# One 128-column projection for the forget gate, the rotary key and its swapped copy

## The chip, the cores and the metric

The kernel runs on one core of a Trainium2 chip. The metric is the device time of one execution in microseconds (us). Before the change three executions took 2214.09, 2215.44 and 2216.43 us; the median is 2215.44 us. The profiled execution took 2216.96 us.

## The reference, cut to what matters

Two networks run one after the other. The first has two layers (`DEPTH = 2`) over 256 tokens of width 1024. Each layer begins like this:

```python
u = rms_norm(x, g_mix[l]) * (1 + sc_a) + sh_a
proj = u @ w_in[l]
fox_qkv, fox_f, mla_ql, mla_kvl, mla_kr, sb_qkv, gate_logit = jnp.split(proj, SPLIT_POINTS, axis=-1)
log_f = jax.nn.log_sigmoid((fox_f + b_fox_f[l]).astype(jnp.float32)).transpose(0, 2, 1)   # 8 columns
y_fox = merge_heads(fox_attention(fq, fk, fv, log_f))      # uses cumsum(log_f) over the tokens
...
k_rope = apply_rope(mla_kr, cos, sin)                      # 32 columns, shared by all 8 heads
y_mla = merge_heads(mla_attention(q_nope, q_rope, k_nope, k_rope, mla_v))
```

`fox_f` has 8 columns and `mla_kr` 32. The rotation is x1*cos - x2*sin next to x1*sin + x2*cos, so the kernel needs `mla_kr` once as it is and once with its two halves swapped. The cumulative sum of `log_f` is first needed by the scores of the first attention; the rotated key is needed by the second attention, later still. The second network (a neighbourhood attention with a gated branch, then a retention layer, each with a feed-forward part) is not touched.

## The kernel before, in words

All weights of both networks lie in HBM as one tape of 518 panels. A panel is 8 tiles of 128x128 float32 (512 KB), in the order in which TensorE uses them. The panels go through a ring of 7 slots (`RING`). For each panel SP issues the DMA once TensorE has released the slot (L912, counter `panel_used`); ScalarE (ACT) copies it to its rounded part `ring_r` (L1468, float32r); VectorE (DVE) computes the rest `ring_l = ring - ring_r` (L2041); then TensorE may use it. The first three panels are rounded and parted by GpSimd (POOL, L927 and L929). One weight tile costs three matmuls of 256 columns: rest times rounded activation, rounded times rounded, rounded times rest of the activation (L969, L972, L973 in `linear`, L1008, L1011, L1012 in `linear_abreast`, L988, L991, L992 with 512 columns in `stream`, which computes the value matrices).

Each engine runs its own instruction list in a fixed order written out by hand. TensorE's groups of one layer are named by `order_block1`; group g writes PSUM bank g mod 8, and waits until the group eight places earlier is freed (`FREED`). A group such as `fox_qk3` is one output tile of 128 features by 256 tokens: 8 weight tiles, so one panel and 24 matmuls.

A layer of the first network starts in this order on TensorE: `fox_f` (8 real columns of its 128, written twice, at partitions 0 and 64), `fox_qk0` and `fox_qk1` abreast, which means that their tiles alternate while the normalised input arrives part by part; `fox_qk2` to `fox_qk7`; `fox_v` (4 panels); `lat0` to `lat4`; `k_rope` (the 32 key columns, four copies side by side); `k_swap` (the same with halves swapped); two short statistics (L1079); `sb_qk0` to `sb_qk7`; `sb_v`; further projections of the latents; then the first scores.

DVE parts the panels in this order of its own: `ahead(name)` parts all panels up to six (`AHEAD`) past the one at which the named group starts. Between them DVE does the adaptive modulation of the next half: `ada` multiplies a 512 KB tile loaded by POOL (L938, two slots) with a vector and sums (L2066). Five of these stand before `fox_v`, four in the `lat` groups, five in the `sb_qk` groups.

For the forget gate ACT takes Abs, Exp and Ln of the bank (L1536, L1539, L1541) at the start of the layer, and DVE adds the bias and clips (L2215) and scans along the tokens (L2219). Both wait for `fox_f` at that place of their lists. In the first layer DVE then computes the rotary angles (L2079 to L2092) and the product of the condition (L2094), which needs ACT's sigmoid of 128x2048 elements (L1472, L1474, L1476); after it ACT loads another table for two sines and loads the first one back. The key is rotated by two products of bank and table (L2200) and one sum (L2203), each on 128 partitions.

ACT copies each finished group out of PSUM (L1514 for the queries and keys, L1554 and L1555 for the latents) and rounds the panels behind it: `finished(name)` waits for a group and rounds the panels that replace what the group before it had read.

Of the kernel before, what the change touches and what calls it, by code (L numbers as in the profile page):

```python
# [32 lines left out]
ACT = mybir.ActivationFunctionType  # L33
ALU = mybir.AluOpType
AX = mybir.AxisListType

P = 128
# [35 lines left out]
FOX_ROWS = 64 + H  # L73
# [4 lines left out]
TILES_1 = (KD + 3 * 4 * KD + KQ * KD + KKV * KD + 2 * KD + 3 * 4 * KD + (4 + 2 + 2) * KQ + 8 * KKV  # L78
           + 3 * KD * KD + 3 * KD * WT + KD * KD + 2 * FT * KD + KD * FT)
PANELS_1 = -(-TILES_1 // TILES_PER_PANEL)  # L80
assert PANELS_1 % RING == 0
# [116 lines left out]
def tape_block1(i, l):  # L198
# [6 lines left out]
    f_pad = np.zeros((D, P), np.float32)  # L205
    f_pad[:, :H] = f_pad[:, 64:FOX_ROWS] = sec[1]
    qk = stationary(sec[0][:, :2 * W])
    out += [abreast(stationary(f_pad), qk[:KD], qk[KD:2 * KD]), qk[2 * KD:], streaming(sec[0][:, 2 * W:])]
# [3 lines left out]
    out += [stationary(np.tile(kr, (1, 4))), stationary(np.tile(kr[:, swap], (1, 4)))]  # L212
# [98 lines left out]
def order_block1():  # L311

    o = ["stat_mix", "fox_f"] + [f"fox_qk{f}" for f in range(2 * WT)] + ["fox_v0", "fox_v1"]
    o += [f"lat{f}" for f in range(KQ + KKV)] + ["k_rope", "k_swap", "stat_q", "stat_kv"]
    o += [f"sb_qk{f}" for f in range(2 * WT)] + ["sb_v0", "sb_v1"]
    o += [f"mla_q{f}" for f in range(WT)] + [f"q_{n}{f}" for n in ("rope", "swap") for f in range(2)]
    o += [f"score{n}" for n in heads(0)]
    o += [f"mla_k{f}" for f in range(WT)] + ["mla_v0", "mla_v1"]
    o += [f"score{n}" for n in heads(1)]
    for p in range(1, PAIRS + 2):  # L320
        if p <= PAIRS:
            o.append(f"gate{2 * p - 2}")
        if p - 1 > STICKS:
            o.append(f"pv{p - 2}")
        if branch_at(p) is not None:
            o += [f"branch{branch_at(p)}_{f}" for f in range(KD)]
        if p <= PAIRS:
            o += [f"keys{n}" for n in heads(p - 1)] + [f"gate{2 * p - 1}"]
        if p + 1 < PAIRS:
            o += [f"score{n}" for n in heads(p + 1)]  # L330
        if p <= STICKS:
            o.append(f"pv{p - 1}")
    o += [f"w_out{f}" for f in range(KD)] + ["stat_ffn"]
    for f in range(FT):
        o += [f"ffn_gate{f}", f"ffn_up{f}"]
    return o + [f"down{f}" for f in range(KD)]
# [41 lines left out]
def two_blocks(nc, tape, ada_first_in, adas, consts, par1, cond_in, pos_in, x_in, par2_in, misc_in, ctx_in, bias_in,  # L378
               sgu_w_in, sgu_b_in, axial, dist_in, mask_in, out):
    n_panels = tape.shape[0]  # L380
    assert n_panels % RING == 0
# [6 lines left out]
    with ExitStack() as ctx:  # L388
# [109 lines left out]
        FOX = place(2 * WT, T)  # L498
        fox_qk, fox_v = at(FOX, 2 * WT, T), carve(2, W)
# [6 lines left out]
        log_keep, log_beta = at(FOX, 4, 3 * P), at(FOX + 12 * P, 4, 3 * P)  # L506
# [110 lines left out]
        cum_made = signal("cum_made", 1)  # L617
# [39 lines left out]
        FREED = {"stat_mix": (log_mean, 0), "fox_f": (fox_low, 0), "k_rope": (rope_mul, 0), "k_swap": (rope_mul, 1),  # L657
# [231 lines left out]
        def _(sp):  # L889
# [18 lines left out]
            with sp.Fori(1, n_panels // RING) as turn:  # L908
                for s in range(RING):
# [3 lines left out]
                        .then_inc(landed[s], 16)  # L913
            quarter = KD // 4
# [8 lines left out]
        def _(pool):  # L923
# [7 lines left out]
            pool.wait_ge(*done("fox_f", 0))  # L931
# [16 lines left out]
        def _(pe):  # L948
# [76 lines left out]
            for l in range(DEPTH):  # L1025
# [89 lines left out]
                project("k_rope", uk)  # L1115
                project("k_swap", uk)
# [13 lines left out]
                def scores(p):  # L1130
# [320 lines left out]
        def _(act):  # L1451
# [9 lines left out]
            def round_panels(n):  # L1461


                while made[0] < n:
                    q = made[0]
                    made[0] += 1
                    act.wait_ge(landed[q % RING], base[0] // RING * 16 + 16 * (q // RING + 1))
# [21 lines left out]
            for l in range(DEPTH):  # L1489
# [35 lines left out]
                if l == 0:  # L1525
# [9 lines left out]
                act.wait_ge(*done("fox_f", l))  # L1535
                act.activation(fox_l[0:FOX_ROWS, :], bank("fox_f")[0:FOX_ROWS, 0:T], ACT.Abs, bias=par_of("b_fox")[0:FOX_ROWS, :])\  # L1536
                    .then_inc(fox_soft.sem, 1)
                act.wait_ge(*fox_soft(0, l))
                act.activation(fox_l[0:FOX_ROWS, :], fox_l[0:FOX_ROWS, :], ACT.Exp, scale=-1.0).then_inc(fox_soft.sem, 1)  # L1539
                act.wait_ge(*fox_soft(1, l))  # L1540
                act.activation(fox_l[0:FOX_ROWS, :], fox_l[0:FOX_ROWS, :], ACT.Ln, bias=1.0).then_inc(fox_soft.sem, 1)  # L1541
                finished("fox_f")
# [14 lines left out]
                finished("k_rope")  # L1557
                finished("k_swap")
# [479 lines left out]
        def _(dve):  # L2038
# [97 lines left out]
            for l in range(DEPTH):  # L2136
# [69 lines left out]
                if l == 0:  # L2206
# [5 lines left out]
                ahead("fox_f", l)  # L2212
                dve.wait_ge(*done("fox_f", l))
                dve.wait_ge(*fox_soft(0, l))
                dve.tensor_scalar(fox_t[0:FOX_ROWS, :], bank("fox_f")[0:FOX_ROWS, 0:T], par_of("b_fox")[0:FOX_ROWS, :], 0.0, ALU.add, ALU.min)\  # L2215
                    .then_inc(fox_low.sem, 1)
                dve.wait_ge(*fox_low(0, l))
                dve.wait_ge(*fox_soft(2, l))
                dve.tensor_tensor_scan(neg_cum[0:FOX_ROWS, :], fox_l[0:FOX_ROWS, :], fox_t[0:FOX_ROWS, :], 0.0, ALU.add, ALU.subtract)\  # L2219
                    .then_inc(cum_made.sem, 1)  # L2220
# [8 lines left out]
                if l == 0:  # L2229
                    rope_angles()  # L2230
# [7 lines left out]
                rotate(0, "k_rope", "k_swap", k_rope)  # L2238
# [612 lines left out]
```

## Time and profile before

| | |
|---|---|
| median of three executions | 2215.44 us |
| profiled execution | 2216.96 us |
| its span, first to last instruction | 2214.9 us |
| outside the span | 2.1 us |
| PE / PEld / DVE / ACT / POOL busy | 2086.2 / 1861.9 / 1601.8 / 1160.1 / 106.8 us |
| instructions PE / DVE / ACT | 13692 / 2625 / 2049 |
| mean granted TensorE clock | 0.979 |
| DMA, tape panels | 518 of 512 KB, median 3.3 us from issue to landing |
| DMA, modulation tiles | 176 of 512 KB, median 4.6 us |

PE is TensorE's matmuls, PEld its weight loads, DVE VectorE, ACT ScalarE, POOL GpSimd, SP SyncE. Matmuls overlap one another, so the duration of one is not its price; the price is the distance between the starts of two. A wait "A <- B" means that A's engine was idle before A and that B ended this. The first layer's projections start at about 40 us and the second's at about 535 us; the first network ends at about 1036 us.

### The profile page before, as it was taken

Reading aid. Unit: us, or ns where it says so; the run is one execution under the profiler, and the core shown is the slowest. Engines: PE = TensorE matmul, PEld = TensorE weight load, DVE = VectorE, ACT = ScalarE, POOL = GpSimd, SP = SyncE. Lnnn points to the kernel's source line nnn. Section 1 sums busy time; section 2 is a strip of 40 time slices with the busy share of each in tenths; the row PEclk is TensorE's granted clock in tenths of the full one; section 3 lists DMA queues with packets and bytes.
Section 4 is the critical chain, followed back from the end, with each engine's and each line's share of the span. In section 5 each row is a group of like instructions: output and inputs, shape, how many; then the busy total and the mean of one; then the engine's idle time right before and its main releaser. Section 6 shows DMA issues by size and latency. Waiting matters only on the chain.

```text
span 2214.9 us, 36264 instructions
## 1 busy us (share of the span) xinstructions
PE 2086.2 (94%) x13692; PEld 1861.9 (84%) x13692; DVE 1601.8 (72%) x2625; ACT 1160.1 (52%) x2049; POOL 106.8 (5%) x186
## 2 busy tenths in 40 slices
PE   3999999999999989998997999999998999998998
PEld 3989999999988989997874668787876888998998
DVE  7778868955778868945876778677877526657983
ACT  3657746645457746645636355353434225656762
POOL 2000000000000000000000100001100000000000
PEclk9999999999999999999998999999999999999999
DMA  8766546854766546855440524546553322243553
GB/s 333 264 232 206 179 159 218 270 189 153 265 225 213 172 162 226 289 170 179 135 162 1 190 86 144 179 133 198 192 190 105 104 95 96 95 144 124 187 185 105
DMA packets 107469, 385.08 MB, mean 174 GB/s; under 512 B 11696, under 2 KB 16432, under 8 KB 106032
## 3 DMA queue, kind: packets, MB, share of 16 engines
q1 hardware_dynamic: 78880, 284.32, 37.9%
q0 software_dynamic: 25344, 92.29, 12.2%
q10 hardware_dynamic: 3088, 6.29, 0.8%
q8 instruction: 109, 1.79, 0.3%
q14 instruction: 48, 0.39, 0.1%
HBM read 381.81 MB, written 1.05 MB: 173 GB/s over the span
## 4 chain that ended last, share of the span: by engine, by line
PE 87%; DVE 7%; ACT 3%; issue 1%; DMA 1%; DVEq 0%; SPq 0%; ACTq 0%
PE ps L969 22%; PE ps L973 22%; PE ps L972 22%; PE ps L988 3%; PE ps L991 3%; PE ps L992 3%; PE ps L1008 2%; PE ps L1011 2%; PE ps L1012 2%; DVE ada_junk L2066 2%; PE ps L1275 1%; PE ps L1418 1%; DVE ring_l L2041 1%; PE ps L1202 1%; DVE work L2467 1%
## 5 line engine op out<-in xcount | busy, mean ns | idle before, releaser
L969 PE MATMUL ps<-part,ring_l 128*128 128x256 f32 (+1 forms) x3568 | 1098.1, 308 | 19.7 <-DVE part L2041 15.4
L973 PE MATMUL ps<-part,ring_r 128*128 128x256 f32 (+1 forms) x3568 | 1084.6, 304 | 0.0
L972 PE MATMUL ps<-part,ring_r 128*128 128x256 f32 (+1 forms) x3568 | 1082.9, 304 | 0.0
L1468 ACT ACTIVATE ring_r<-ring 128x1024 fp32r<-128x1024 f32 x515 | 535.4, 1057 | 450.1 <-DMA ring<-tape_in 332.1
L2041 DVE TENSOR_TENSOR ring_l<-ring,ring_r 128x1024 fp32r<-128x1024 f32 x515 | 622.2, 1220 | 195.8 <-ACT ring_r L1468 193.1
L969 PEld LDWEIGHTS ps<-part,ring_l 128*128 128x128 f32 x3568 | 672.8, 189 | 62.3 <-DVE part L2041 20.2
L972 PEld LDWEIGHTS ps<-part,ring_r 128*128 128x128 f32 x3568 | 675.6, 189 | 30.4 <-issue 1.2
L973 PEld LDWEIGHTS ps<-part,ring_r 128*128 128x128 f32 x3568 | 671.8, 188 | 28.8
L2066 DVE SCALAR_TENSOR_TENSOR ada_junk<-work 128x1024 bf16<-128x1024 f32 x272 | 337.7, 1242 | 49.2 <-DMA work<-adas_in 36.8
L1008 PE MATMUL ps<-part,ring_l 128*128 128x256 f32 (+1 forms) x240 | 79.6, 332 | 35.4 <-DVE part L2185 20.9
L988 PE MATMUL ps<-ring_l,part 128*128 128x512 f32 x264 | 105.3, 399 | 6.0 <-DVE part L2456 6.0
L991 PE MATMUL ps<-ring_r,part 128*128 128x512 f32 x264 | 104.8, 397 | 0.0
L992 PE MATMUL ps<-ring_r,part 128*128 128x512 f32 x264 | 104.7, 397 | 0.0
L2491 DVE SCALAR_TENSOR_TENSOR work<-ps,par,work 128x510 f32<-128x510 f32 (+1 forms) x88 | 53.9, 612 | 55.7 <-ACT work L1789 55.4
L938 POOL DMA_DIRECT2D work<-adas_in x96 | 50.9, 530 | 853.2 <-DVE ada_junk L2066 823.6
L1008 PEld LDWEIGHTS ps<-part,ring_l 128*128 128x128 f32 x240 | 51.2, 213 | 41.9 <-issue 39.6
L1789 ACT ACTIVATE work<-ps,par 128x512 f32<-128x512 f32 (+1 forms) x88 | 58.0, 660 | 42.7 <-PE ps L973 29.6
L1011 PE MATMUL ps<-part,ring_r 128*128 128x256 f32 (+1 forms) x240 | 78.0, 325 | 0.0
L1012 PE MATMUL ps<-part,ring_r 128*128 128x256 f32 (+1 forms) x240 | 78.0, 325 | 0.0
L944 POOL DMA_DIRECT2D work<-adas_in x80 | 42.3, 529 | 689.0 <-DVE ada_junk L2066 689.0
L2041 DVE TENSOR_TENSOR part<-work,part 128x256 fp32r<-128x256 f32 (+1 forms) x134 | 61.4, 470 | 10.1 <-ACT part L1926 3.9
L1476 ACT ACTIVATE work<-work 128x256 f32<-128x256 f32 (+2 forms) x138 | 64.6, 468 | 4.4
(226 smaller groups left out, 1947.7 us busy)
## 6 DMA issues: line engine op xcount, KB each, us to landing
ring<-tape_in SPq DMA_DIRECT2D x518, 512.0 KB, 3.3
work<-adas_in POOLq DMA_DIRECT2D x176, 512.0 KB, 4.6
work<-ada_first_in SPq DMA_DIRECT2D x8, 1024.0 KB, 13.2
work<-bias_in ACTq DMA_DIRECT2D x1, 2048.0 KB, 7.9
x<-x_t_in SPq DMA_DIRECT2D x1, 1024.0 KB, 15.6
work<-cond_in SPq DMA_DIRECT2D x1, 1024.0 KB, 18.2
x<-ctx_in ACTq DMA_DIRECT2D x1, 1024.0 KB, 7.6
x<-dist_in ACTq DMA_DIRECT2D x1, 1024.0 KB, 9.7
```

The source lines that it names most:

```text
L969: mm = pe.matmul(dst, lhsT=wl, rhs=mr, start=(k == 0), stop=False)
L972: pe.matmul(dst, lhsT=wr, rhs=mr, start=False, stop=False)
L973: mm = pe.matmul(dst, lhsT=wr, rhs=ml, start=False, stop=(k == len(moving) - 1))
L988: mm = pe.matmul(dst, lhsT=xr, rhs=wl, start=(k == 0), stop=False)
L991: pe.matmul(dst, lhsT=xr, rhs=wr, start=False, stop=False)
L992: mm = pe.matmul(dst, lhsT=xl, rhs=wr, start=False, stop=(k == n - 1))
L1008: mm = pe.matmul(dst, lhsT=wl, rhs=mr, start=(k == 0), stop=False)
L1011: pe.matmul(dst, lhsT=wr, rhs=mr, start=False, stop=False)
L1012: mm = pe.matmul(dst, lhsT=wr, rhs=ml, start=False, stop=(k == len(moving) - 1))
L1468: act.activation(ring_r[:, q % RING, :], ring[:, q % RING, :], ACT.Copy).then_inc(rounded, 1)
L2041: return dve.tensor_tensor(dst, whole, rounded_part.bitcast(F32), ALU.subtract)
L2066: dve.scalar_tensor_tensor(ada_junk[:, :], t, 1.0, vector, ALU.mult, ALU.mult, accum_out=sums).then_inc(sig.sem, 1)
```

## The change

`fox_f`, `k_rope` and `k_swap` become one group, `fox_rope`, that stands where `k_rope` stood. Its 128 columns are the key (0 to 31), the swapped key (32 to 63) and the forget gate (64 to 71); the rest is zero. `fox_qk0`, `fox_qk1` and `fox_qk2` now run abreast. The work of ACT and DVE on the forget gate moves behind the `lat` groups, and DVE rotates 32 partitions instead of 128 and adds four times, once for each copy of the result. The scanned row block of partitions 64 to 71 is copied to partitions 0 to 7. A layer has 145 panels in place of 147, so the tape has 514, no multiple of 7; the last three are issued behind SP's loop, and a slot's number follows from the whole tape and not from the layer.

```diff
-    out += [abreast(stationary(f_pad), qk[:KD], qk[KD:2 * KD]), qk[2 * KD:], streaming(sec[0][:, 2 * W:])]
+    out += [abreast(*(qk[f * KD:(f + 1) * KD] for f in range(ABREAST))), qk[ABREAST * KD:], streaming(sec[0][:, 2 * W:])]
-    out += [stationary(np.tile(kr, (1, 4))), stationary(np.tile(kr[:, swap], (1, 4)))]
+    fox_rope = np.zeros((D, P), np.float32)
+    fox_rope[:, 0:ROPE], fox_rope[:, ROPE:2 * ROPE], fox_rope[:, FOX] = kr, kr[:, swap], sec[1]
+    out += [stationary(fox_rope)]
...
-    o = ["stat_mix", "fox_f"] + [f"fox_qk{f}" for f in range(2 * WT)] + ["fox_v0", "fox_v1"]
-    o += [f"lat{f}" for f in range(KQ + KKV)] + ["k_rope", "k_swap", "stat_q", "stat_kv"]
+    o = ["stat_mix"] + [f"fox_qk{f}" for f in range(2 * WT)] + ["fox_v0", "fox_v1"]
+    o += [f"lat{f}" for f in range(KQ + KKV)] + ["fox_rope", "stat_q", "stat_kv"]
...
-        FREED = {"stat_mix": (log_mean, 0), "fox_f": (fox_low, 0), "k_rope": (rope_mul, 0), "k_swap": (rope_mul, 1),
+        FREED = {"stat_mix": (log_mean, 0), "fox_rope": (rope_mul, 1),
...
+            for n in range(n_panels // RING * RING, n_panels):                       # SP
+                sp.wait_ge(panel_used, n - RING + 1)
+                sp.dma_start(ring[:, n % RING, :], tape[n]).then_inc(landed[n % RING], 16)
...
-            pool.wait_ge(*done("fox_f", 0))
+            pool.wait_ge(*done("fox_qk0", 0))
...
-                slot = panel % RING                                                  # PE
+                slot = (base[0] + panel) % RING
...
-                project_abreast(["fox_f", "fox_qk0", "fox_qk1"], uk, lambda k: u_made(k, l))
-                for f in range(2, 2 * WT):
+                project_abreast([f"fox_qk{f}" for f in range(ABREAST)], uk, lambda k: u_made(k, l))
+                for f in range(ABREAST, 2 * WT):
                     project(f"fox_qk{f}", uk)
...
-                project("k_rope", uk)
-                project("k_swap", uk)
+                project("fox_rope", uk)
...
-                        pe.wait_ge(*cum_made(0, l))
+                        pe.wait_ge(*cum_made(1, l))
...
+                act.wait_ge(*done("fox_rope", l))          # ACT, behind lat4; Abs, Exp, Ln moved here
+                act.activation(fox_l[FOX, :], bank("fox_rope")[FOX, 0:T], ACT.Abs, bias=par_of("b_fox")[FOX, :])\
...
-                ahead("fox_f", l)                          # DVE, start of the layer; clip and scan moved
-                dve.wait_ge(*done("fox_f", l))
+                ahead("fox_qk0", l)
+                if l == 0:
+                    rope_angles()
...
-                rotate(0, "k_rope", "k_swap", k_rope)
+                ahead("fox_rope", l)
+                dve.wait_ge(*done("fox_rope", l))
+                dve.wait_ge(*fox_soft(0, l))
+                dve.tensor_scalar(fox_t[FOX, :], bank("fox_rope")[FOX, 0:T], par_of("b_fox")[FOX, :], 0.0, ALU.add, ALU.min)\
...
+                dve.tensor_tensor_scan(neg_cum[FOX, :], fox_l[FOX, :], fox_t[FOX, :], 0.0, ALU.add, ALU.subtract)\
...
+                dve.tensor_copy(neg_cum[0:H, :], neg_cum[FOX, :]).then_inc(cum_made.sem, 1)
+                straight, swapped, first = slice(0, ROPE), slice(ROPE, 2 * ROPE), bank("fox_rope")
+                dve.tensor_tensor(rope_t[straight, 0, :], first[straight, 0:T], rope_c[straight, :], ALU.mult).then_inc(rope_mul.sem, 1)
+                dve.tensor_tensor(rope_t[straight, 1, :], first[swapped, 0:T], rope_s[swapped, :], ALU.mult).then_inc(rope_mul.sem, 1)
+                dve.wait_ge(*rope_mul(1, l))
+                for n in range(4):
+                    add = dve.tensor_tensor(k_rope[n * ROPE:(n + 1) * ROPE, :], rope_t[straight, 0, :], rope_t[straight, 1, :], ALU.add)
+                add.then_inc(rope_made.sem, 1)
```

## Rows read from the trace of the kernel before

**Rows 1.** The page: busy time, and the engines of the chain that ended last.
```profile
PE 2086.2 (94%) x13692; PEld 1861.9 (84%) x13692; DVE 1601.8 (72%) x2625; ACT 1160.1 (52%) x2049; POOL 106.8 (5%) x186
...
PE 87%; DVE 7%; ACT 3%; issue 1%; DMA 1%; DVEq 0%; SPq 0%; ACTq 0%
```

**Rows 2.** Stretches: length; busy and instructions by engine; granted clock, DMA share, GB/s.
```profile
core 0: us, PE busy (x) PEld busy (x) DVE busy (x) ACT busy (x) POOL busy (x), PEclk, DMA share, GB/s
50.18:69.21 19.03, 17.67 (x146) 17.39 (x145) 14.80 (x22) 18.41 (x23) 1.51 (x3) 1.00 0.61 224
80.44:100.59 20.15, 20.15 (x170) 20.15 (x168) 15.65 (x19) 12.65 (x20) 2.08 (x4) 1.00 0.84 287
...
546.74:564.02 17.28, 17.28 (x146) 17.28 (x145) 12.72 (x15) 9.03 (x16) 1.58 (x3) 1.00 0.71 242
575.26:595.41 20.15, 20.15 (x169) 20.15 (x168) 14.46 (x18) 12.43 (x20) 1.98 (x4) 1.00 0.75 258
160.00:200.00 40.00, 39.70 (x327) 34.30 (x326) 36.74 (x86) 32.74 (x88) 3.70 (x7) 1.00 0.63 205
```

**Rows 3.** TensorE's waits from 40 to 300 us: total, times, longest.
```profile
PE ps L1202 <- DVE work L2330: 1.4, 1, 1.4
PE ps L969 <- DVE ring_l L2041: 1.4, 1, 1.4
```

**Rows 4.** Waits of all engines, 40 to 205 us.
```profile
ACT ring_r L1468 <- DMA ring<-tape_in: 13.0, 10, 2.8
...
DVE ada_junk L2066 <- DMA work<-adas_in: 8.0, 8, 2.1
DVE work L2192 <- PE ps L992: 6.6, 1, 6.6
```

**Rows 5.** Timeline of PE, ACT and DVE, 43 to 62 us: start, us, instruction, [idle before].
```profile
60.34 0.36 PE L969 MATMUL ps<-part,ring_l 128*128 128x256 f32 x1 [1.36 <-DVE ring_l L2041]
...
43.98 3.89 ACT L1468 ACTIVATE ring_r<-ring 128x1024 fp32r<-128x1024 f32 x4
...
50.93 1.90 ACT L1472 ACTIVATE work<-work 128x2048 f32<-128x2048 f32 x1
...
56.75 1.28 ACT L1547 ACT_TABLE_LOAD   x1
...
60.09 0.94 ACT L1514 ACTIVATE work<-ps 128x256 f32<-128x256 f32 x3
...
50.23 0.48 DVE L2215 TENSOR_SCALAR work<-ps,par 72x256 f32<-72x256 f32 x1 [1.60 <-ACT work L1536]
51.13 0.69 DVE L2219 TENSOR_TENSOR_SCAN work<-work 72x256 f32<-72x256 f32 x1 [0.42 <-ACT work L1541]
...
56.77 2.29 DVE L2094 TENSOR_TENSOR work<-work 128x2048 f32<-128x2048 f32 x1 [1.68 <-ACT work L1476]
58.98 1.22 DVE L2041 TENSOR_TENSOR ring_l<-ring,ring_r 128x1024 fp32r<-128x1024 f32 x1
62.00 1.23 DVE L2041 TENSOR_TENSOR ring_l<-ring,ring_r 128x1024 fp32r<-128x1024 f32 x1 [1.81 <-ACT ring_r L1468]
```

**Rows 6.** Timeline of DVE around the end of the values, and at the next ones.
```profile
77.88 1.23 DVE L2066 SCALAR_TENSOR_TENSOR ada_junk<-work 128x1024 bf16<-128x1024 f32 x1 [0.68 <-DMA work<-adas_in]
...
80.08 1.23 DVE L2041 TENSOR_TENSOR ring_l<-ring,ring_r 128x1024 fp32r<-128x1024 f32 x1
...
98.56 1.22 DVE L2066 SCALAR_TENSOR_TENSOR ada_junk<-work 128x1024 bf16<-128x1024 f32 x1 [1.39 <-DMA work<-adas_in]
```

**Rows 7.** DVE by line and shape, 40 to 150 us: count, busy us, mean ns, idle before.
```profile
L2041 DVE TENSOR_TENSOR ring_l<-ring,ring_r 128x1024 fp32r<-128x1024 f32 x37 | 44.3, 1221 | 7.7 <-ACT ring_r L1468 7.5
...
L2203 DVE TENSOR_TENSOR work<-work 128x256 f32<-128x256 f32 x3 | 1.3, 426 | 0.1
...
L2200 DVE TENSOR_TENSOR work<-ps,rope_c 128x256 f32<-128x256 f32 x3 | 1.3, 419 | 0.1
```

**Rows 8.** The stretch that follows a wait of TensorE of 1.4 us.
```profile
290.00:300.00 10.00, 9.05 (x63) 8.74 (x64) 5.84 (x11) 3.06 (x5) 0.02 (x1) 0.83 0.43 151
```

More of the change, by code:

```diff
@@ L72 @@
 STICKS = 2 * PER_BRANCH
-FOX_ROWS = 64 + H
+FOX = slice(64, 64 + H)
 ADA_BEFORE = {"fox_qk": 5, "lat": 4, "sb_qk": 5, "q_rope": 2}
@@ L380, in two_blocks @@
     n_panels = tape.shape[0]
-    assert n_panels % RING == 0
     cat, n_const = columns(shape_constants())
@@ L497, in two_blocks @@
         HIDDEN = taken[0]
-        FOX = place(2 * WT, T)
-        fox_qk, fox_v = at(FOX, 2 * WT, T), carve(2, W)
+        FOX_QK = place(2 * WT, T)
+        fox_qk, fox_v = at(FOX_QK, 2 * WT, T), carve(2, W)
         sb_qk, sb_v = carve(2 * WT, T), carve(2, W)
@@ L505, in two_blocks @@
         soft = at(LAT, 4, 3 * P)
-        log_keep, log_beta = at(FOX, 4, 3 * P), at(FOX + 12 * P, 4, 3 * P)
+        log_keep, log_beta = at(FOX_QK, 4, 3 * P), at(FOX_QK + 12 * P, 4, 3 * P)
         sigma = carve(SIGMAS, T)
@@ L616, in two_blocks @@
         fox_low = signal("fox_low", 1)
-        cum_made = signal("cum_made", 1)
+        cum_made = signal("cum_made", 2)
         qk_made = signal("qk_made", 4 * WT)
@@ L1464, in round_panels @@
                 while made[0] < n:
-                    q = made[0]
+                    q = base[0] + made[0]
                     made[0] += 1
-                    act.wait_ge(landed[q % RING], base[0] // RING * 16 + 16 * (q // RING + 1))
+                    act.wait_ge(landed[q % RING], 16 * (q // RING + 1))
                     act.activation(ring_r[:, q % RING, :], ring[:, q % RING, :], ACT.Copy).then_inc(rounded, 1)
@@ L1532, in _ @@
                 round_panels(RING)
[L1535 to L1542, printed above, removed]
                 if l == 0:
@@ L1556, in _ @@
                     finished(f"lat{f}")
-                finished("k_rope")
-                finished("k_swap")
+                act.wait_ge(*done("fox_rope", l))
+                act.activation(fox_l[FOX, :], bank("fox_rope")[FOX, 0:T], ACT.Abs, bias=par_of("b_fox")[FOX, :])\
+                    .then_inc(fox_soft.sem, 1)
+                act.wait_ge(*fox_soft(0, l))
+                act.activation(fox_l[FOX, :], fox_l[FOX, :], ACT.Exp, scale=-1.0).then_inc(fox_soft.sem, 1)
+                act.wait_ge(*fox_soft(1, l))
+                act.activation(fox_l[FOX, :], fox_l[FOX, :], ACT.Ln, bias=1.0).then_inc(fox_soft.sem, 1)
+                finished("fox_rope")
                 inverse_rms(1, "stat_q", MLA_Q, l)
@@ L2209, in _ @@
                 normalised(0, gs_mix, 0)
-                ahead("fox_f", l)
-                dve.wait_ge(*done("fox_f", l))
[L2214 to L2220, printed above, removed]
+                ahead("fox_qk0", l)
+                if l == 0:
+                    rope_angles()
                 ada_next = itertools.count()
@@ L2811 @@
             par1[:, l, a:a + w] = feature_major(v[l])
-        par1[:H, l, PAR1["b_fox"][0]] = par1[64:FOX_ROWS, l, PAR1["b_fox"][0]] = i["b_fox_f"][l]
+        par1[FOX, l, PAR1["b_fox"][0]] = i["b_fox_f"][l]
     par2 = np.zeros((P, DEPTH, N_PAR2), np.float32)
```

12 lines of the change are left out of this document (6 added, 6 removed).

## The prediction

> **What bounds the kernel now.** I read the page first: TensorE has matmuls in flight for 94% of the span, and 87% of the chain that ended last is PE [rows 1]. A busy PE can still be a slow one, because matmuls overlap, so I looked next at the stretches in which the three groups lie. From 80.44 to 100.59 us TensorE runs `lat0` to `lat4`, `k_rope` and `k_swap`: 7 groups of 24 matmuls, 168 in all (the row counts two that reach in). PE and PEld are busy for the whole 20.15 us. The same seven groups of the second layer take 20.15 us again [rows 2]. That is 2.879 us a group, or 119.9 ns from one matmul to the next, with two quite different DVE and DMA shares beside it. So in this part time is the number of matmuls times 120 ns, and nothing else.
>
> The queries and keys behind the abreast part (`fox_qk2` to `fox_qk7`) are 144 matmuls. In the second layer they take 17.28 us, 2.880 us a group. In the first they take 19.03 us less a gap of 0.12 to the next line, so 1.6 us more, and PE is busy for 17.67 us only [rows 2]. The waits say why: one of 1.4 us at L969 for a `ring_l` of DVE; between 40 and 290 us there is no other wait above 1 us inside the projections [rows 3]. Everything else that DVE, ACT and the DMAs do there is behind TensorE. DVE even stands 6.6 us waiting for the `sb_v` matmuls [rows 4].
>
> **The matmuls that go.** Per layer 24 tiles (`fox_f`, `k_rope`, `k_swap`) become 8. That is 16 tiles, 48 matmuls, two panels; twice, 96 matmuls and four panels. One group leaves ahead of `fox_v`: the abreast part keeps three groups and its pace is that of the arriving input, so the group is missing in the 120 ns part behind it, which has five groups in place of six. The other leaves behind `lat4`. Saved: 4 groups x 2.879 us = 11.5 us [rows 2]. The Trainium skill (TensorE: Matmul & The Clock Gate, Back-to-back issue gap) gives 262 cycles of 2.4 GHz, 109 ns, for an isolated gap of 256 columns; by it the 96 matmuls would be worth 10.5 us. The trace has 119.9 ns at the full clock, and the measurement decides.
>
> **The wait at 60.34 us in the first layer.** Its history is in the timeline [rows 5]. DVE clips and scans the forget gate from 50.23 to 51.82 us after standing 1.60 us for ACT's Abs and 0.42 us for the Ln; it computes the angles until 55.09; it stands 1.68 us for the sigmoid of the condition, which ACT could start only at 50.93, behind Abs, Exp and Ln; the product takes 2.29 us; only then, at 58.98, is panel 6 parted, until 60.20. TensorE wanted it at 50.18 + 3 x 2.88 = 58.8 us and got it at 60.34. The lost time is 1.5 us.
> After the change ACT is done with its four panels at 43.98 + 3.89 = 47.9 us and goes straight to the sigmoid, which takes 56.75 - 50.93 = 5.8 us, so until 53.7. DVE has its angles by then (3.3 us from 48.6). Product until 56.0, panel 6 until 57.2: 1.6 us ahead of need. What is late next is panel 7, for whose rounding DVE stands 1.81 us now too. ACT must first change tables and do the sines (60.09 - 56.75 = 3.3 us, to 57.0), then copy four groups instead of three (0.31 each, to 58.3), round panel 7 (1.0) and DVE part it (1.2): about 60.5, wanted at 61.7. Margin 1.2 us. Behind it the five modulation tiles come. The first starts 3.6 us earlier than now and each later one hangs on the landing of a load that the one before it let POOL issue, so the last ends 3.6 us earlier, at 75.5 instead of 79.1 [rows 6], while TensorE is 1.5 + 2.9 = 4.4 us earlier. The parting now at 80.08 to 81.3 serves a panel wanted at 83.3, so 2.0 us of margin become about 1.2. I count the full 1.5 us as saved; from the other side it is 0, if one of the two margins of 1.2 us is gone.
>
> **The forget gate and the rotation, moved and reshaped.** On ACT the three operations cost what they cost before, and two roundings of 1.05 us go. On DVE, per layer: two partings of 1.22 go (2.44 us), and of the rotation nothing but the number of adds changes, from one to four, plus one copy. No row shows an operation on 32 or 8 partitions. The nearest are the add on 128 partitions (0.426 us) and the clip on 72 (0.480 us) [rows 5, 7]; from below it is nothing, from above 0.69 us, the scan's. I take 0.43, as partitions seem not to enter: the clip on 72 costs no less than the product on 128 (0.419). So four operations more make 1.7 us, against 2.4 saved: DVE has 0.7 us less to do per layer (bounds: 2.4 less to 0.4 more). None of it stands on the path.
> But the block is one piece now: clip 0.48, scan 0.69, copy 0.43, two products 0.84, four adds 1.70, in all 4.1 us, and a wait for TensorE and ACT in front. Behind it in DVE's list stand all later partings, the normalisation of the latents and the `sb_qk` modulation tiles. `ahead("fox_rope")` has parted up to five panels past the group before, 5 x 2.88 = 14.4 us of work for TensorE. And DVE comes late: its last modulation tile in the `lat` groups ends now at 99.8 us [rows 6], 2.1 us after `k_rope` (97.7); after the change it moves up by 4 to 5 us, with two partings behind it, so the block begins some 4 us after `fox_rope` is finished. ACT is through with Abs, Exp and Ln by then (1.4 us [rows 5], behind one rounding). I cost the wait at nothing and the block at nothing. The lag this adds to DVE, some 4 us, is worked off in the 6.6 us in which it now waits for `sb_v` [rows 4]. The cumulative sum is needed at the first score, over 40 us later; if this cover were gone the price would be the block's 4.1 us.
>
> **The rest.** POOL's first modulation load waits for `fox_qk0` instead of `fox_f`, both the first group of the abreast part: nothing. SP's three loose issues are behind the same counter as in the loop: nothing. The banks turn by two places, but the distance of eight groups to the one freed is kept everywhere, and near the merged group the freed ones are over four groups (11 us) old: nothing. 2 MB of 385 less to load: nothing, as no transfer is on the path here.
>
> **Sum.** 11.5 + 1.5 = 13.0 us. Everything after the first scores is tied to TensorE and moves up with it. Against the profiled 2216.96 us (span 2214.9 and 2.1 around it) this is 2204.0; that execution is 1.5 us above the median, and against the median of 2215.44 it is 2202.4. I forecast 2202.4 us.
>
> **The rivals.**
> *The wait only moves.* The first layer's 1.5 us come back at panel 7 or behind the values, because both margins are 1.2 us and rest on landings that now vary (waits of DVE for modulation tiles up to 2.1 us [rows 4]). For it: ACT is busy for 18.41 of 19.03 us in that stretch [rows 2]. Then only the matmuls count: 2215.4 - 11.5 = 2203.9; with a new stall of 2 us in each layer, 2208.
> *Another engine has become the bound further on.* Between 160 and 200 us DVE is busy for 36.74 of 40 us [rows 2]. If it set the pace there, TensorE's lead would be lost in a wait, and only DVE's own saving, 0.7 us a layer, and part of the 1.5 would stay: 2213 to 2214, no change. Against it: PE waits 0.3 us in those 40 (39.70 busy), and DVE catches up with TensorE at `sb_v`, before this part.
> *The clock.* After the wait of 1.4 us near 290 us the granted clock is 0.83 over ten microseconds [rows 8], that is 3.4 us at 1.2 GHz in place of 2.4, which costs 1.7 us. Such stretches begin and end a few microseconds apart from run to run; a wait that goes can save one, a new one can add one: 1.7 us either way. It widens the range.
> *Slower: the moved block starves TensorE.* ACT's list is in order: the Abs stands behind roundings that wait for landings (2.8 us the longest here [rows 4]), DVE's block behind the Abs, the partings behind the block. It decides once DVE stands longer than the 14.4 us of parted panels. Every microsecond beyond that is lost in both layers; 6.5 us beyond cancel the gain, and at 25 us of standing, 10.6 lost per layer and a slow clock after each (1.7), the time is 2202.4 + 2 x 12.3 = 2227. Against it: the longest wait seen plus the whole block and ACT's three operations is 2.8 + 4.1 + 1.4 = 8.3 us.
> *The change doesn't do what it says.* If the compiled tape kept 518 panels, nothing would be saved; the trace would show 13692 matmuls again. I see no place where this could come from.
>
> **How the numbers follow.** Forecast, 2200.5 to 2204.5 by the spread of the three runs and the clock: 0.68. The wait moves, 2203.9 to 2208: 0.20. Absorbed further on or not made, 2211 to 2215: 0.05. More than forecast, to 2198, by slow-clock stretches that go: 0.05. Slower: 0.02. The range that holds 8 in 10 is 2199.5 to 2206.5; the bounds of DVE's small operations do not widen it, as they are covered. About 0.2%, 4.4 us, is what a measurement of this kernel tells from no change. Faster by more: 0.93; within: 0.05; slower: 0.02.
>
> **What would show it.** Matmuls 13596, panels 514. The run behind the abreast part is five groups long and takes 14.4 us in both layers, with no wait at L969; the run from `lat0` to the statistics takes 17.3 us. The first layer's `fox_v` starts 4.4 us earlier, the statistics 7.3 us earlier than at 100.59; the second layer's are 13 us earlier than at 595.4. DVE's block begins after `fox_rope` has ended and without idle time before the clip. The prediction is wrong if PE shows a wait above 1 us between 50 and 140 us, if the lead of 7 us at the statistics is smaller at the first `gate` groups, or if the groups cost other than 2.88 us.

## The result, and the profile after

The changed kernel took 2203.67 us (median of 6 executions) and the kernel before 2215.93 us (6) on the same chip. The ratio is 0.9933 with a 95% interval of 0.9913 to 0.9952: 14.8 us less, between 10.6 and 19.3. One disturbed execution of the changed kernel, far above the rest (2957.66 us), is left out of the ratio but stands among the 6; without it the median is 2202.98. The changed kernel was run twice more beside the experiments: 2202.08 us, ratio 0.9933 (0.9912 to 0.9955), and 2203.23 us, ratio 0.9946 (0.9927 to 0.9965). The forecast was 2202.4 us, 13.0 less than before. An interval of 10.6 to 19.3 us contains that, but it contains 11.5 as well; which terms are right has to come from the traces.

The changed kernel's page, the lines that answer to [rows 1], and its panels:

```profile
PE 2081.3 (94%) x13596; PEld 1856.5 (84%) x13596; DVE 1601.9 (72%) x2629; ACT 1156.6 (52%) x2045; POOL 107.0 (5%) x186
...
PE 86%; DVE 8%; ACT 3%; issue 1%; DMA 1%; DVEq 0%; SPq 0%; ACTq 0%
...
ring<-tape_in SPq DMA_DIRECT2D x514, 512.0 KB, 3.4
```

96 matmuls are gone, and PE is busy for only 4.9 us less than in [rows 1]. The clock of the two profiled executions hides the rest: the third profile of the changed kernel, which has a mean clock of 0.980, shows PE busy for 2072.8 us, 13.4 less than before. A mean granted clock of 0.979 over a span of 2214.9 us means 93 us at 1.2 GHz in place of 2.4. If the work of these 93 us were done in half of them at the higher level, some 47 us would be lost to the clock. The profile of after has 0.975:

```profile
core 0: 2210.4 us, clock 0.975
```

Summed over the single stretches, the profile of before has 93.1 us at the lower level and that of after 110.0. Half of it taken off each span leaves 2168.3 and 2155.4 us, which is 12.9 less. This is rough, and that it comes out so near the forecast is in part luck: the other two profiles of the changed kernel give 2150.9 (where 2155 was expected) and 2155.0 us by the same sum. It takes too much off every span, for two reasons. The part of such a stretch in which TensorE is idle costs nothing. And in the projections matmuls at 1.2 GHz start 213 ns apart in place of 119.9 (in the run with 48 further adds, below), so a busy stretch loses 44% of its length, not half.

So the profiled execution of after (2212.49 us) lies 9 us above the median of its kernel, and the spans alone would have told of a third of the gain.

The stretches of the projections in the changed kernel, each layer's run behind the abreast part and its `lat` groups with `fox_rope`, as in [rows 2]: length; busy and instructions by engine; granted clock, DMA share, GB/s.

```profile
51.31:65.70 14.39, 14.39 (x123) 14.39 (x121) 10.57 (x12) 13.27 (x19) 1.99 (x4) 1.00 0.76 260
76.95:94.22 17.27, 17.27 (x145) 17.27 (x144) 13.22 (x16) 11.16 (x19) 1.59 (x3) 1.00 0.76 254
538.90:553.30 14.40, 14.40 (x122) 14.40 (x121) 6.92 (x8) 7.14 (x12) 1.06 (x2) 1.00 0.67 225
564.50:581.80 17.30, 17.30 (x145) 17.25 (x144) 12.72 (x15) 11.95 (x19) 1.59 (x3) 1.00 0.79 269
```

PE is busy for the whole length of all four. The first has shrunk from 19.03 us to 14.39: a group and the wait. The `lat` runs are 2.88 us shorter, one group.

TensorE's waits of after between 40 and 300 us (total, times, longest) answer to [rows 3]:

```profile
PE ps L1009 <- DVE part L2183: 10.8, 1, 10.8
PE ps L970 <- DVE part L2039: 1.6, 2, 0.9
PE ps L1202 <- DVE work L2337: 1.4, 1, 1.4
PE ps L1202 <- ACT work L1596: 0.3, 1, 0.3
```

The wait for `ring_l` is gone. The first row is the start of the layer, where TensorE waits for the normalised input. The second row is two waits for a `part` of the activations, further on in the layer: 0.9 us at 285.59, which the kernel before has too (0.9 at 291.82), and 0.7 us at 299.52, which it has not. The second profile of the changed kernel does not have the 0.7 us, so they are not a fixed part of the change.

### The profile page after: what moved, and what is told of

Same layout as the page of the kernel before. It is cut to its first block, busy times and chain, and to the rows that moved or that the text cites. A ratio compares the mean times of both kernels' runs of the same rounds, so it can differ in the third digit from the quotient of the medians.

```text
span 2210.4 us, 36038 instructions
## 1 busy us (share of the span) xinstructions
PE 2081.3 (94%) x13596; PEld 1856.5 (84%) x13596; DVE 1601.9 (72%) x2629; ACT 1156.6 (52%) x2045; POOL 107.0 (5%) x186
## 3 DMA queue, kind: packets, MB, share of 16 engines
q0 software_dynamic: 25344, 92.29, 12.3%
## 4 chain that ended last, share of the span: by engine, by line
PE 86%; DVE 8%; ACT 3%; issue 1%; DMA 1%; DVEq 0%; SPq 0%; ACTq 0%
PE ps L970 22%; PE ps L974 22%; PE ps L973 22%; PE ps L989 3%; PE ps L992 3%; PE ps L993 3%; PE ps L1009 2%; PE ps L1012 2%; PE ps L1013 2%; DVE ada_junk L2064 2%; PE ps L1418 1%; PE ps L1275 1%; DMA ring<-tape_in 1%; DVE ring_l L2039 1%; ACT ring_r L1468 1%
```

## The experiments

Each was timed beside the kernel before on the same chip; its ratio is to that. Differences between two variants are differences of medians, good to some 4 us; the changed kernel's medians are 2202.08 to 2203.67 us. It was timed beside the three longer blocks and the first two kernels that fill waits, but not beside the first four experiments or the last one. The first four undo a part of the change or do one alone.

**48 matmuls a layer put back, their panels not.** TensorE goes over the panel of `fox_rope` twice more before the real pass; the results of the extra passes are overwritten.

```diff
+                again = open_bank("fox_rope")[:, 0:T]
+                for _ in range(2):
+                    for k, (mr, ml) in enumerate(uk):
+                        ...                              # the three matmuls of a tile, from the panel that fox_rope reads
                 project("fox_rope", uk)
```

> The changed kernel, but TensorE computes the merged group three times over, two times for nothing and then for good, on the same panel. So it has the 13692 matmuls of the kernel before and only the 514 panels of the new one; the two empty passes put 48 matmuls a layer between lat4 and the statistics. Theory (the price is the number of matmuls, 119.9 ns each, 11.5 us in all; 1.5 us come from the wait in the first layer that is gone): 11.5 us slower than the changed kernel, that is 1 to 2 us under the kernel before, about 2214; the run from lat0 to the statistics takes 28.8 - 5.8 = 23.0 us with 192 matmuls in both layers. Rival (what was saved is the load, rounding and parting of four panels, and the matmuls were partly hidden): it stays near 2203.

2218.17 us (12 executions), ratio 1.0002 (0.9984 to 1.002). The whole gain is gone, with 514 panels on the tape and no wait for a panel. The 1.5 us of the wait, which should have stayed, do not show in the time, whose interval reaches 4 us either way. The `lat` run of the first layer:

```profile
77.12:100.15 23.03, 23.03 (x193) 23.03 (x192) 17.36 (x20) 11.93 (x19) 2.12 (x4) 1.00 0.75 259
```

192 matmuls in 23.03 us are 119.9 ns each, the price in [rows 2], although two of the eight panels are not loaded. So it is the matmuls that cost here, not what feeds them.

**Two panels a layer put back, without their matmuls.** The panels are loaded, rounded and parted, and released by one matmul each (four in all).

```diff
-    out += [stationary(fox_rope)]
+    out += [np.zeros((2 * KD, P, P), np.float32), stationary(fox_rope)]
...
+                for _ in range(2):
+                    wr, wl, ends = take(TILES_PER_PANEL)
...
+                    pe.matmul(idle, lhsT=wl[:, 0:TILE], rhs=u_r[:, 0, :], start=True, stop=True).then_inc(panel_used, 1)
```

> The changed kernel, but each layer has two more panels of zeros ahead of the merged group. They are loaded, rounded and parted like the others, and TensorE spends one matmul on each to release it. So DMA, ACT and DVE have the 518 panels of the kernel before, TensorE 13600 matmuls. Theory: nothing but the four matmuls, 0.5 us: about 2203 to 2204. Its one risk is that the ring of seven slots passes three panels within 3.1 us there, so TensorE may wait behind lat4 for a panel that is loaded only once another is released; the parted lead of five panels should hide it. Rival (panels are what costs, 2.9 us each): 11.5 us more, about 2214.

2207.61 us (12), ratio 0.9965 (0.9949 to 0.998). A good part of the gain stays: 9.9 us by the medians, where the changed kernel has 12.3, and 7.8 (4.4 to 11.3) by the ratio, where that has 14.8. It is 4 to 5.5 us above the changed kernel where 0.5 was expected; the 11.5 us of the rival on record are excluded. One wait of TensorE is longer, in the second layer, 1.6 us where the three profiles of the changed kernel have 0.3 to 0.5 at that place (L1178 there):

```profile
PE ps L1184 <- DVE work L2306: 1.6, 1, 1.6
```

The first layer's `lat` run, with the two extra panels, has no loss in it: 147 matmuls in 17.51 us.

```profile
76.50:94.01 17.51, 17.51 (x147) 17.51 (x146) 14.20 (x17) 12.05 (x19) 1.69 (x4) 1.00 0.83 293
```

Where the other 2 to 4 us are is open; they are within what the comparison can miss. With half of the time at 1.2 GHz taken off, its span is 2155.7 us, which is that of the changed kernel's first profile (2155.4), so the trace shows no place for them. That panels cost nothing at all isn't shown; that they cost much less than their matmuls is.

**Only the order.** All three groups are kept and stand behind `lat4`, so that the forget gate has left the start of the layer and nothing is merged.

```diff
+    o = ["stat_mix"] + [f"fox_qk{f}" for f in range(2 * WT)] + ["fox_v0", "fox_v1"]
+    o += [f"lat{f}" for f in range(KQ + KKV)] + ["fox_f", "k_rope", "k_swap", "stat_q", "stat_kv"]
```

> The move without the merger: three groups again, forget gate, key and swapped key, all three behind lat4, with fox_qk0 to fox_qk2 abreast and the work of ACT and DVE on the forget gate behind the lat groups. 13692 matmuls, 518 panels, rotation on 128 partitions as before. Theory: only the wait at 60 us goes, 1.5 us: about 2214; the profile shows no wait of TensorE in the queries of the first layer and 25.9 us minus nothing for the 192 matmuls behind the values, that is 23.0 us for eight groups. Rival (the new order is what pays): most of the 13 us, about 2204.

2215.61 us (12), ratio 0.9998 (0.9983 to 1.0012): 1.9 us under the median before. The times can't tell such a difference from none. The trace can: the run behind the abreast part is free of the wait, and the `lat` run is the eight groups long that it should be.

```profile
50.81:65.21 14.40, 14.40 (x122) 14.40 (x121) 10.60 (x13) 13.69 (x19) 1.58 (x4) 1.00 0.74 259
76.45:99.49 23.04, 23.04 (x193) 23.04 (x192) 20.09 (x28) 14.21 (x23) 2.64 (x5) 1.00 0.87 296
```

**Only the keys merged.** The forget gate is computed at the start of the layer as before; key and swapped key share a group.

```diff
-    out += [abreast(*(qk[f * KD:(f + 1) * KD] for f in range(ABREAST))), qk[ABREAST * KD:], ...]
+    out += [abreast(stationary(f_pad), qk[:KD], qk[KD:2 * KD]), qk[2 * KD:], ...]
```

> Half of the merger without the move: the forget gate keeps its own group, abreast with two query groups at the start of the layer, and its place in the lists of ACT and DVE; key and swapped key share one group. 13644 matmuls, 516 panels. Theory: 48 matmuls at 119.9 ns, 5.8 us less than before, about 2210, and the wait of 1.4 us at 60 us is there again. Rival (the gain is that of the move): no change, 2215.

2214.17 us (12), ratio 0.998 (0.9958 to 1.0001), 3.4 us under the median before, where 48 matmuls are worth 5.8. Taken to one clock as above, the profiled spans differ by 5.8, a sum that is good to a few us. The wait is back at its old place, as it must be if the forget gate's chain on ACT and DVE causes it (compare [rows 5]):

```profile
60.89 0.36 PE L972 MATMUL ps<-part,ring_l 128*128 128x256 f32 x1 [1.37 <-DVE ring_l L2042]
```

**How much cover does the moved block have?** The changed kernel's trace shows no wait behind the block, so the cover had to be found by making the block longer: 12, 24 or 48 further adds of 32 partitions in front of the last four, each 0.445 us with the wait for the one before it.

```diff
                 dve.wait_ge(*rope_mul(1, l))
+                for n in range(24):
+                    dve.tensor_tensor(k_rope[straight, :], rope_t[straight, 0, :], rope_t[straight, 1, :], ALU.add).then_inc(fox_low.sem, 1)
+                    dve.wait_ge(*fox_low(n + 1, l))
                 for n in range(4):
                     add = dve.tensor_tensor(k_rope[n * ROPE:(n + 1) * ROPE, :], ...)
```

> DVE's block longer by 12 adds that wait for one another, 5.3 us per layer, below the cover of 6.6 and 7.3 us that the block of 24 has measured (there TensorE waited 3.7 and 4.0 us for 10.6 us more). Theory A: no wait at L970 in the sb_qk part and the time of the changed kernel, within 1.5 us. Rival (any lag of DVE costs, by a later wait further on in the layer): 2 us or more per layer.

2205.15 us (6), ratio 0.9948 (0.993 to 0.9967), beside 2203.23 for the changed kernel timed with it. 5.3 us more of DVE's time in each layer cost nothing that can be measured; the longest wait of TensorE for a panel is 0.2 us, at `sb_v` of the first layer:

```profile
PE ps L989 <- DVE ring_l L2039: 0.2, 1, 0.2
```

> The changed kernel with DVE's block made longer: 24 further adds of 32x256, each waiting for the one before, between the products and the four adds, some 0.44 us each, 10.6 us per layer; nothing else in the kernel waits for them. As the trace of the changed kernel has it, DVE parts panel 23 right behind the block, at 102.8 to 104.0 us, and TensorE wants it at 96.2 + 5 x 2.88 = 110.6, so 6.6 us of cover in the first layer; in the second 591.0 against 598.3, 7.3 us. Theory A (this margin is the cover, since DVE reaches the block 4 us late): TensorE waits 4.0 and 3.3 us at L970 in the sb_qk part, and with a slow stretch of the clock after each the time is 8 to 12 us over the changed kernel, about 2213 to 2216. Theory B, the prediction's (five panels, 14.4 us, are the cover): the block with its additions is 14.7 us, so nothing or under 1 us: 2204.

2217.07 us (12), ratio 1.0003 (0.9989 to 1.0018). DVE behind `fox_rope` in the first layer, and then TensorE's wait in the first layer (100 to 140 us) and in the second (590 to 630 us):

```profile
100.92 10.69 DVE L2244 TENSOR_TENSOR work<-work 32x256 f32<-32x256 f32 x24
111.64 1.70 DVE L2247 TENSOR_TENSOR work<-work 32x256 f32<-32x256 f32 x4
113.37 1.23 DVE L2039 TENSOR_TENSOR ring_l<-ring,ring_r 128x1024 fp32r<-128x1024 f32 x1
```

```profile
PE ps L970 <- DVE ring_l L2039: 3.7, 1, 3.7
```

```profile
PE ps L970 <- DVE ring_l L2039: 4.0, 1, 4.0
```

10.7 us more make waits of 3.7 and 4.0, so 7.0 and 6.7 us were covered. The prediction's cover, five panels, would have given no wait or one under 1 us. The time is 15.0 us above the changed kernel's 2202.08 beside it, more than the 7.7 of the waits. The granted clock falls at 114.1 us, 0.7 us before the first wait ends, and is back at 120.9: 6.2 us of work with 213 ns from one matmul to the next in place of 119.9, 2.7 us lost. The stretch behind the second wait is 3.4 us long, 1.5 us lost. That makes 11.9 of the 15.0; the other 3 are open and within what the medians can miss.

> As e6, with 48 further adds: 21.1 us per layer. Theory A (cover 6.6 and 7.3 us): waits of 14.5 and 13.8 us, and a slow stretch after each, 30 to 36 us over the changed kernel: about 2234 to 2240; the later part of the layer may keep a part of DVE's lag, as DVE is busy for nine tenths there. Theory B (cover 14.4): 10.8 us a layer in all: about 2226.

2236.08 us (6), ratio 1.0098 (1.0075 to 1.012), 34 us above the changed kernel. The waits are 14.4 and 14.6 us, 10.7 and 10.6 more than with 24 adds: beyond the cover each microsecond of DVE is one of TensorE. The clock is down for 17.1 us at each, from 112.8 to 129.9 us at the first, but TensorE is idle there until 124.8; only the 5.0 us behind the wait are work, 2.2 us lost. At the second it is 5.7 us of work (629.3 to 635.0), 2.5 lost. With the 29.0 us of the waits that makes 33.7, and 34.0 was measured. The first wait's end with the distance of two matmuls at the lower level, and the stretch around it with PE busy for 5.64 of 20 us:

```profile
124.83 0.55 PE L970 MATMUL ps<-part,ring_l 128*128 128x256 f32 x1 [14.36 <-DVE ring_l L2039]
...
127.53 0.41 PE L970 MATMUL ps<-part,ring_l 128*128 128x256 f32 x1
127.74 0.41 PE L973 MATMUL ps<-part,ring_r 128*128 128x256 f32 x1
127.95 0.41 PE L974 MATMUL ps<-part,ring_r 128*128 128x256 f32 x1
```

```profile
110.00:130.00 20.00, 5.64 (x29) 5.46 (x29) 19.00 (x42) 4.89 (x11) 0.43 (x1) 0.57 0.10 31
```

**The clock at the start of a layer.** Both kernels run part of the abreast groups at 1.2 GHz, after TensorE has waited for the normalised input. Three kernels fill that wait with matmuls of constants whose results nothing uses. The edit of the second:

```diff
+            def stay_busy(bank, n):
+                for _ in range(n):
+                    pe.matmul(bank[:, 0:T], lhsT=const("ones"), rhs=cst[:, 0:T], start=True, stop=True)
...
+                stay_busy(open_bank(f"fox_qk{2 * WT - 4}"), 10 if l == 0 else 6)
                 project_abreast([f"fox_qk{f}" for f in range(ABREAST)], uk, lambda k: u_made(k, l))
```

The first has them only there (18 in layer 0, 6 in layer 1):

> The changed kernel, and TensorE is kept at work in the two gaps ahead of the first projections of a layer: 18 float32 matmuls of 256 columns (36 in the trace) before the first layer's, 6 (12) before the second's, into a bank that is free; their results are not used. In the changed kernel the abreast parts of 72 matmuls take 11.05 and 11.34 us, the first at the lower clock from 40.25 to 45.5 us, the second from 527.7 to 533.7. Theory (the difference between two runs of one kernel is the time at 1.2 GHz, half of which is lost where TensorE is the bound): both abreast parts run at 2.4 GHz from the start and take about 9 us each, unless the arriving input sets the pace: 3 to 5 us under the changed kernel, about 2200. Rival (the input sets the pace of the abreast parts, or the dummies end too late and push the start): no gain, 2204 or a microsecond or two more.

2210.41 us (11), ratio 0.9966 (0.9947 to 0.9985), 8.3 us above the changed kernel's 2202.08 beside it, where 3 to 5 under it were expected. The matmuls in the first layer opened a bank that DVE frees at 37.5 us only; the abreast part began behind them at 48.11 in place of 40.2, 7.9 us late, as the rival on record had it. In the second layer the abreast part ran at 2.4 GHz throughout and took 8.7 us (534.34 to 543.03 us), against 11.2 in two profiles of the changed kernel (527.70 to 538.92 in the first) and 10.1 in the other.

The second has 10 in the first layer and others of the kind in front of the first network's feed-forward part and of three places of the second network:

> e8 with the first gap filled to its length and four kinds of gap more. In e8 the 18 float32 matmuls ahead of the first layer ended at 48.1 us, 7.9 us after the input was ready, because most of them ran at 1.2 GHz; ahead of the second layer 6 of them took 2.6 of the 3.3 us, no slow stretch followed, and the abreast part took 8.7 us where the changed kernel needed 10.1 to 11.3. Here: 10 ahead of the first layer, 6 ahead of the second, 6 ahead of each first feed-forward part, 9 ahead of the wide feed-forward and of the retention queries, 6 ahead of the last feed-forward part. Results of these matmuls are not used. Theory (half of each slow stretch is lost where TensorE is the bound, and it follows on the gap): 1.2 to 2.5 us at each of seven places, 8 to 15 us under the changed kernel, about 2188 to 2194, and the share of the clock at 0.985 or above. Rival (the input sets the pace after the gaps): not over 3 us.

2199.35 us (6), ratio 0.9917 (0.9896 to 0.9937): 3.9 us under the changed kernel's 2203.23 beside it, where 8 to 15 were expected. The start of the second layer's abreast part, in the changed kernel and then in this one:

```profile
527.00:540.00 13.00, 12.60 (x83) 12.63 (x84) 10.61 (x18) 6.49 (x12) 0.00 (x0) 0.76 0.28 88
```

```profile
530.00:543.00 13.00, 12.67 (x102) 12.22 (x101) 11.33 (x20) 7.21 (x14) 0.00 (x0) 1.00 0.36 122
```

The granted clock is 1.00 in place of 0.76, and 102 matmuls, four of them the last fillers, fit where 83 did. In the first layer the fillers (each counts as two) are late again and push the start of the abreast part to 45.0 us:

```profile
37.75 7.61 PE L1024 MATMUL ps<-cst 128*128 128x256 f32 x20 [9.09 <-DVE ada_sums L2119]
```

The third writes the first layer's fillers (13) to a bank that is free early and so waits for nothing:

```diff
-                stay_busy(open_bank(f"fox_qk{2 * WT - 4}"), 10 if l == 0 else 6)
+                stay_busy(open_bank(f"fox_qk{2 * WT - 4}") if l else bank(f"fox_qk{2 * WT - 4}"), 6 if l else 13)
```

> e9, with the matmuls ahead of the first layer freed of a wait. In e9 these 10 stood behind the wait that a bank's opening brings, for DVE's ada_sums at 37.5 us, began at 37.75 and ended at 45.0, 4.8 us after the input was ready at 40.2. The bank is unused there, so here 13 of them start right behind the first statistics, at 28.3 us, and should end by 39 us. All else as e9; results of these matmuls are not used. Theory (e9's late start costs 4.8 us and what the other places give back is kept): 4 to 6 us under e9, 10 to 12 us under the changed kernel, about 2193; the first abreast part starts at 40.2 and takes 8.7 us. Rival (DVE, which has more panels to part in less time once the abreast part is short, becomes the bound in the first layer, as it was before the change): the queries show a wait of TensorE of 1 us or more near 58 us, and the time is 2195 or more.

2195.36 us (5), ratio 0.9902 (0.9885 to 0.9918). It beats both kernels: some 22 us under the one before by its ratio, and 7 to 8 under the changed one by the medians, none of which was taken beside it.

```profile
core 0: 2192.4 us, clock 0.987
```

Its 56 us at 1.2 GHz stand against 90 to 110 in three profiles of the changed kernel. Of the 10 to 12 us hoped for it gave less. In the first layer the fillers ended at 34.4 us, TensorE then stood for 6 us until 40.37, and the clock was down from 37.3 to 44.1 all the same, so the abreast part took 10.2 us and not 8.7. That is 1.5 us of the shortfall. The rest fits a price of the clock that was taken too high, though no run separates it: against the third profile of the changed kernel the span is 7.4 us shorter for 34 us less at 1.2 GHz, a fifth and not half. The rival's sign, a wait of 1 us or more near 58 us, is absent.

## Why the prediction was right, step by step

**The matmuls, 11.5 us: right.** 120 matmuls take 14.39 us and 144 take 17.27, 119.9 ns each, in both layers. The 262 cycles (109 ns) that the Trainium skill gives for an isolated gap of 256 columns (TensorE: Matmul & The Clock Gate, Back-to-back issue gap) would have made 10.5 us, an estimate from that page. The measured distance decides: three lengths of run, 120, 144 and 192 matmuls, give 119.9. Putting the matmuls back alone returned the kernel to its old time, and putting the panels back alone did not: 7.8 to 9.9 us of the gain stayed.

**The wait at 60.34 us, 1.5 us: right.** It is absent from the changed kernel and from the one with the order alone, and present in the one that keeps the forget gate at the start. What came instead in the changed kernel, on ACT and then on DVE:

```profile
47.80 1.91 ACT L1472 ACTIVATE work<-work 128x2048 f32<-128x2048 f32 x1
...
53.63 1.28 ACT L1539 ACT_TABLE_LOAD   x1
...
58.03 2.97 ACT L1468 ACTIVATE ring_r<-ring 128x1024 fp32r<-128x1024 f32 x3
```

```profile
53.64 2.29 DVE L2092 TENSOR_TENSOR work<-work 128x2048 f32<-128x2048 f32 x1 [1.70 <-ACT work L1476]
55.85 1.22 DVE L2039 TENSOR_TENSOR ring_l<-ring,ring_r 128x1024 fp32r<-128x1024 f32 x1
59.15 2.36 DVE L2039 TENSOR_TENSOR ring_l<-ring,ring_r 128x1024 fp32r<-128x1024 f32 x2 [2.08 <-ACT ring_r L1468]
```

The sigmoid began at 47.80 (said: 47.9), the product at 53.64 (53.7), panel 6 was parted at 57.07 (57.2) and panel 7 at about 60.4 (60.5). In this execution the run began 1.1 us later than before, at 51.31, as the clock rose later, so panel 7 was wanted at 62.8 and the margin was 2.4 us; from the old start, 50.18, it would have been 1.3, where 1.2 was said. The second margin, behind the values, also said to be 1.2, was 2.4 here (parted at 77.41, used at 79.83) and 1.9 in the third profile, whose run began at 51.12. So both margins held, each helped by about a microsecond by the late start. The 1.5 us are read from the traces; no time here is sharp enough to show them.

**The block on DVE, hidden: right, but its cover was mis-sized.** DVE behind `fox_rope`:

```profile
96.27 2.35 DVE L2039 TENSOR_TENSOR ring_l<-ring,ring_r 128x1024 fp32r<-128x1024 f32 x2
98.65 0.48 DVE L2231 TENSOR_SCALAR work<-ps,par 8x256 f32<-8x256 f32 x1
99.17 0.68 DVE L2235 TENSOR_TENSOR_SCAN work<-work 8x256 f32<-8x256 f32 x1
99.89 0.28 DVE L2238 COPY work<-work 8x256 f32<-8x256 f32 x1
100.20 0.41 DVE L2240 TENSOR_TENSOR work<-ps,rope_c 32x256 f32<-32x256 f32 x1
100.64 0.42 DVE L2241 TENSOR_TENSOR work<-ps,rope_s 32x256 f32<-32x256 f32 x1
101.09 1.70 DVE L2244 TENSOR_TENSOR work<-work 32x256 f32<-32x256 f32 x4
102.83 1.23 DVE L2039 TENSOR_TENSOR ring_l<-ring,ring_r 128x1024 fp32r<-128x1024 f32 x1
```

It begins 4.4 us after `fox_rope` (94.2), without idle time before the clip, and ends 4.2 us later; 4 and 4.1 were said. Only the copy is off, 0.28 for 0.43. But the step that set the point at which it would begin to cost said that DVE might stand for 14.4 us, five panels. The experiments put it at 6.7 to 7.0 us beyond what the block takes, 10.9 to 11.2 us in all. The sum that was wanted counts three more terms. TensorE finds five parted panels and the two short statistics ahead, so it runs from 94.2 until 96.2 + 14.4 = 110.6 us. Of these 16.4 us DVE's own lag takes 4.4, the block 4.2, and the first parting behind it 1.2: 6.6 remain. The prediction compared its 8.3 us with 14.4 and left out lag and parting; with them the conclusion holds, but the reserve is 2.6 to 2.9 us and not 6.1. The prediction's outcome "slower" would begin some 3 us of standing earlier than it said.

**DVE's lag is worked off at `sb_v`: right.** Its wait there was 6.6 us [rows 4] and is 5.0 now:

```profile
DVE work L2190 <- PE ps L993: 5.0, 1, 5.0
```

**The rest, nothing: right as far as it could be seen.** Roundings of ACT now wait for landings 16 times, 19.3 us in total, against 10 times and 13.0 us [rows 4], as TensorE releases the slots faster; no wait of TensorE for a panel hangs on it. Two small waits are there that the kernel before hasn't: the 0.7 us at 299.52, and 0.3 to 0.5 us at L1178 in the second layer in all three profiles. They are part of what was put at nothing.

**The lead is kept: nearly, and in part by luck.** `fox_v` starts 3.5 us earlier (65.70 for 69.21), where 4.4 was said. The 7.3 us of the first layer's statistics read 6.4 in the profile (94.22 for 100.59), as the abreast part ended a microsecond late. At the first `gate` group, where the prediction would have called a smaller lead its failure, it is 6.4 still (149.45 for 155.81). The second layer's statistics begin at 581.96 us, 13.45 before the 595.41 of before (13 was said). But the way there is another: the late microsecond was made good by 1.5 us near 292 us, where the kernel before has 3.4 us at 1.2 GHz [rows 8] and this execution of the changed one has none. The second profile of the changed kernel has such a stretch there. The prediction had a slow stretch as a possible gain, priced at 1.7 us. The second network starts 12.2 us earlier (1027.57, 1039.78). Behind that the slower clock of this one execution ate most of the lead.

**The rivals.** None of the first two came: neither margin was used up, and no other engine had become the bound between 160 and 200 us, where PE is now busy for all of the 40 us. The clock was rightly a term of the range and not of the sum, but it was counted too small: 1.7 us either way was said, and between single executions of one kernel the mean clock goes from 0.975 to 0.981 and the time by 16 us (2196.1 to 2212.49). Medians of six take most of that out.

## What to carry to other kernels

Where PE and PEld are busy for the whole of a stretch, a padded group costs its full number of matmuls, whatever it holds: merging mostly empty tiles saves exactly that number times the distance of two starts. Before a block is moved behind a group on another engine, count its cover as panels ready, less that engine's lag, less the block, less the first operation that feeds TensorE again, and check it with a block made longer. A profiled execution says where time goes, but its span alone told of a third of this gain. Taking half of the time at 1.2 GHz off both helps, but three profiles of one kernel still lie 4.5 us apart by that sum; to price a part of a change, follow the lead of one matmul over the same matmul of the kernel before.

## What had not been expected of the hardware

- DVE operations on few partitions cost nearly what they cost on many, which the prediction assumed and no row before showed: the add 0.415 us on 32 partitions and 0.426 on 128 [rows 7], the clip 0.48 on 8 and 0.48 on 72 [rows 5], the scan 0.68 on 8 and 0.69 on 72.
- At the lower clock these projections lose less than half: matmuls of 256 columns start 213 ns apart at 1.2 GHz and 119.9 at 2.4.
- A wait of TensorE costs more than its length, but not in proportion to it: behind 14.4 us of waiting it worked for 5.0 us at 1.2 GHz, behind 3.7 us for 6.2. The 14.4 us themselves, mostly at the lower level, lost nothing more.
- Matmuls of constants in a wait keep the granted clock at 1.00 (the second layer's abreast part in 8.7 us in place of 10.1 to 11.2), if they reach to the end of the wait; 6 us of idle time behind them were enough to lose it.
